# Feed-forward inputs turned and summed in another order, and the opening's Strassen sums taken from turned quarters, in a two-block transformer kernel

## What is computed

```python
def first_block(x, ...):
    h = rms_norm(x, norm_mix); proj = h @ w_in       # 5888 columns: attention, retention, gates
    ...                                              # windowed attention and chunked retention
    x = x + merged @ w_out
    h = rms_norm(x, norm_ffn)
    x = x + (silu(h @ w_gate) * (h @ w_up)) @ w_down # 2816 wide
    return rms_norm(x, final_norm)

def hybrid_layer(x, ...):
    ...                                              # dilated attention and spatial gating
    x = x + rms_norm_2(mix, g_post_mix)
    h = rms_norm_2(x, g_pre_ffn)
    f = jnp.square(jax.nn.relu(h @ w_ff1)) @ w_ff2   # 4096 wide
    return x + rms_norm_2(f, g_post_ffn)
```

## Time and profile before

| | us |
|---|---|
| median of 3 runs | 2594.77 |
| lowest and highest | 2594.12 and 2595.74 |
| the profiled execution | 2595.17 |
| its span in the trace | 2593.3 |
| PE busy | 2550.8 |
| DVE, POOL, ACT busy | 1585.5, 1246.0, 1052.7 |

### The profile page before, as it was taken

How to read it: one execution, slowest core, us unless ns; L and a number is a source line. 1 busy time by engine, 2 the same in 40 slices (tenths; PEclk the granted TensorE clock), 3 DMA queues, 4 the chain that set the end, 5 groups by cost and what they waited for, 6 DMA issues and landing times. The chain is left out here.

```text
span 2593.3 us, 35295 instructions
## 1 busy us (share of the span) xinstructions
PE 2550.8 (98%) x13038; PEld 2127.8 (82%) x13038; DVE 1585.5 (61%) x2592; ACT 1052.7 (41%) x2081; POOL 1246.0 (48%) x994
## 2 busy tenths in 40 slices
PE   8999999999999999999999999999998999999998
PEld 6888888677888888888888878998888888888886
DVE  7355554685536554454698761168658666587787
ACT  4332343584224332232444551169744322254443
POOL 2479784354525665555221774548545544200204
PEclk9999999999999999999999999999999999999999
DMA  5557674705551222222752344323143333364534
GB/s 216 193 185 284 223 263 155 276 18 190 187 184 66 74 89 90 79 77 72 284 191 94 110 151 180 89 65 86 51 132 106 114 106 112 118 250 134 184 102 166
DMA packets 162710, 372.40 MB, mean 144 GB/s; under 512 B 21538, under 2 KB 42658, under 8 KB 158882
## 3 DMA queue, kind: packets, MB, share of 16 engines
q1 hardware_dynamic: 162540, 370.15, 41.5%
HBM read 268.01 MB, written 101.83 MB: 143 GB/s over the span
## 5 line engine op out<-in xcount | busy, mean ns | idle before, releaser
L2353 POOL TENSOR_TENSOR WL<-WRAW,WH 128x512 fp32r<-128x512 f32 (+1 forms) x149 | 247.7, 1664 | 277.2 <-ACT WH L1098 277.1
L852 PE MATMUL PS<-HH,WL 128*128 128x512 f32 (+1 forms) x976 | 368.5, 378 | 2.6 <-DVE HL L1881 0.9
L854 PE MATMUL PS<-HL,WH 128*128 128x512 f32 (+1 forms) x976 | 366.7, 376 | 0.0
L855 PE MATMUL PS<-HH,WH 128*128 128x512 f32 (+1 forms) x976 | 366.6, 376 | 0.0
L1619 DVE TENSOR_TENSOR WL<-TS,WH 128x512 fp32r<-128x512 f32 x228 | 245.6, 1086 | 193.1 <-ACT WH L1098 193.0
L917 PE MATMUL PS<-WH,DAL 128*128 128x512 f32 x756 | 294.7, 390 | 0.0
L919 PE MATMUL PS<-WH,DAH 128*128 128x512 f32 x756 | 294.5, 390 | 0.0
L918 PE MATMUL PS<-WL,DAH 128*128 128x512 f32 x756 | 294.5, 390 | 0.0
L2532 POOL TENSOR_TENSOR X<-X,DV 128x512 f32<-128x512 f32 x56 | 90.1, 1633 | 354.4 <-DVE DV L2024 270.3
L1098 ACT ACTIVATE WH<-TS 128x512 fp32r<-128x512 f32 x228 | 138.3, 621 | 213.9 <-POOL TS L2369 213.8
L2369 POOL TENSOR_TENSOR TS<-WRAW 128x512 f32<-128x512 f32 x114 | 153.2, 1344 | 129.8 <-issue 122.6
(11 more groups left out here) (418 smaller groups left out, 6070.0 us busy)
## 6 DMA issues: line engine op xcount, KB each, us to landing
WRAW<-in_u_f SPq DMA_DIRECT2D x56, 512.0 KB, 3.9
WRAW<-in_u_in SPq DMA_DIRECT2D x54, 512.0 KB, 4.4
WRAW<-scr_t SPq DMA_DIRECT2D x52, 512.0 KB, 3.7
scr_h<-HS SPq DMA_DIRECT2D x96, 256.0 KB, 2.2
WRAW<-in_u_gu SPq DMA_DIRECT2D x44, 512.0 KB, 3.4
scr_t<-TTa SPq DMA_DIRECT2D x18, 1024.0 KB, 4.1
WRAW<-in_u_out SPq DMA_DIRECT2D x24, 512.0 KB, 3.5
scr_x<-X SPq DMA_DIRECT2D x24, 512.0 KB, 4.9
```

What stands on the lines that cost most here:

```text
L852: e.matmul(PS[:, b, 0:wd], wl[:, blk(kk)], op_moving(q, kk, c0, wd, 0), start=(kk == 0), stop=False)
L854: e.matmul(PS[:, b, 0:wd], wh[:, blk(kk)], op_moving(q, kk, c0, wd, 1), start=False, stop=False)
L855: mm = e.matmul(PS[:, b, 0:wd], wh[:, blk(kk)], op_moving(q, kk, c0, wd, 0), start=False, stop=(kk == 3))
L2353: e.tensor_tensor(lo, raw, hi.bitcast(F32), ALU.subtract).then_inc(*c.inc("w_lo_p", i))
```

## The change

In the opening the sixteen transposed sum tiles and turn0 go. POOL writes the whole (high plus low) of the turned quarters of rows 0 to 3 back over X (whole_rows, at i = 0 and 1, behind the low part of weight unit 6); DVE's sums0 forms S3 and S2 from them and from the PSUM banks of the turned rows 4 to 7, which it now frees (before, the split of the row did); POOL forms S4 and S1 at i = 6 to 9; ACT and DVE split the four sums from X, in SBUF, at i = 4 to 15.

In both feed-forward openings four groups (j = 2) move ahead of the first product and the other four (j = 3) to P2 (two), P4 and P3 of block (0, 0). ACT's high parts of the sums are taken out of turn and put in a list of their own, HIGH_TERMS. DVE runs two of the four early groups before the norm of the first block's last row and two after P1, ahead of the low part of the seventh weight operand. POOL's low parts move a little earlier. In the second opening ACT, in place of DVE, squares the quarters of pairs 0 and 1.

```diff
+    HIGH_AT = {4: [("S3", 0), ("S2", 0)], 5: [("S3", 1), ("S2", 1)], 6: [("S3", 2), ("S2", 2)], 7: [("S3", 3), ("S2", 3)],
+               9: [("S4", 0)], 10: [("S4", 1)], 11: [("S4", 2)], 12: [("S4", 3)],
+               13: [("S1", 0)], 14: [("S1", 1)], 15: [("S1", 2), ("S1", 3)]}
+    LOW_AT = HIGH_AT
...
-    AFTER_OUT = {7: 2, 8: 2, 9: 2, 10: 2}
-    AFTER_PROD = {0: [0, 1, 1, 1, 1, 0, 1], 1: [1, 1, 1, 0, 0, 0, 0]}
+    AFTER_OUT = {7: 2, 8: 2, 9: 2, 10: 2, 15: 4}
+    AFTER_PROD = {0: [0, 0, 0, 0, 2, 1, 1], 1: [0] * 7}
...
-    LOW_PROD = {0: [0, 0, 0, 1, 1, 1, 1], 1: [0, 1, 1, 1, 1, 0, 0]}
+    LOW_PROD = {0: [0, 0, 1, 1, 2, 0, 0], 1: [2, 2, 0, 0, 0, 0, 0]}
+    HIGH_TERMS = [(q, j) for j in range(4) for q in ("S1", "S3", "S2", "S4")]
+    HIGH_OUT = {8: 4, 10: 4}
+    HIGH_PROD = {0: [4, 0, 0, 0, 0, 1, 3], 1: [0] * 7}
+    SUMS_OUT = {**AFTER_OUT, 15: 2}
+    SUMS_PROD = {0: [2, 0, 0, 0, 2, 1, 1], 1: [0] * 7}
...
 PE, opening:
-        def turn0(q, j):
-            b = open_bank(("nb", 1, q, j))
-            w.wait_ge(*c.at("s_ov", (1, j, "S4")))
-            for i in range(4):
-                mm = e.transpose(PS[:, b, blk(i)], by_tile(rows0(q, j))[:, i, :], ID[:, :])
-            mm.then_inc(*bk.fill(("nb", 1, q, j)))
...
 ACT, opening:
+        def high_term(q, j):
+            if q == "S4":
+                w.wait_ge(*c.at("s_op", (1, j, "S1")))
+            if q == "S1":
+                w.wait_ge(*bk.full(("rv", 1, j + 4)))
+            w.wait_ge(*sum0_done(q, j))
+            e.activation(op_cols(q, j, 0), whole0(q, j), ACT.Copy).then_inc(*c.inc("h_hi", (1, q, j)))
...
 ACT, second feed-forward:
+        def squared(m, c0, wd, p):
+            t = quarter(2, m, DONE[p])[:, c0:c0 + wd]
+            w.wait_ge(*bk.out((p, 2, m, c0)))
+            e.activation(t, t, ACT.Relu).then_inc(*c.inc("f_r", (m, c0, p)))
+            w.wait_ge(*c.at("f_r", (m, c0, p)))
+            e.activation(t, t, ACT.Square).then_inc(*c.inc("f_s", (m, c0, p)))
...
                     if c0 == 0 and m in AFTER_PROD:
                         turns(k, backs, AFTER_PROD[m][x])
+                        high_terms(k, highs, HIGH_PROD[m][x])
                         if m == 0:
                             split()
+                    if lay == 2 and m < 2 and p in ("P4", "P3"):
+                        squared(m, c0, wd, "P5" if p == "P4" else "P4")
+                        if p == "P3":
+                            squared(m, c0, wd, "P3")
...
 DVE, opening:
+            key = "nb", 1, j + 4, 0
+            for q, b2, left, right in (("S3", 0, whole0("A11", j), None), ("S2", 1, None, whole0("S3", j))):
+                key = "nb", 1, j + 4, b2
+                ps = by_tile(PS[:, bk.at(key), :])
+                e.tensor_tensor(whole0(q, j), ps if left is None else left, ps if right is None else right,
+                                ALU.subtract).then_inc(*bk.free(key))
...
 DVE, first feed-forward:
+            if i == 15:
+                turns(2, backs, SUMS_OUT[i])
             if i in COMPLETE:
                 w.wait_ge(*c.at("gb0", 2))
                 norm(2, tt, GF[:, :])
-            turns(2, backs, AFTER_OUT.get(i, 0))
+            if i < 15:
+                turns(2, backs, SUMS_OUT.get(i, 0))
...
 DVE, second feed-forward:
-                    if lay == 2 and p in ("P5", "P4", "P3"):
+                    if lay == 2 and m >= 2 and p in ("P5", "P4", "P3"):
...
                     if c0 == 0 and m in AFTER_PROD:
-                        turns(k, backs, AFTER_PROD[m][x])
                         if also and m == 0:
                             also(x)
+                        turns(k, backs, SUMS_PROD[m][x])
...
 POOL, opening:
+        def whole_rows(tt):
+            for half in range(2):
+                hh, hl = [t[:, 4 * half:4 * half + 4, blk(tt)].bitcast(F32) for t in (HH, HL)]
+                w.wait_ge(*bk.out(("nb", 1, tt, half)))
+                w.wait_ge(*bk.full(("nb", 1, tt, 1)))
+                e.tensor_tensor(whole0(("A11", "A12")[half], tt), hh, hl, ALU.add).then_inc(*c.inc("s_op", (tt, half)))
...
+            if i < 2:
+                whole_rows(2 * i)
+                whole_rows(2 * i + 1)
+            if 6 <= i < 10:
+                sums0(i - 6)
```

More of the change, by code:

```diff
@@ L611, in op_done @@
     def op_done(k, q, j):
-        return c.at("s_op", (k, q, j)) if k > 1 and q[0] == "S" else bk.out(("nb", k, q, j))
+        if q[0] == "A":
+            return bk.out(("nb", k, q, j))
+        return c.at("s_ov", ("lo", q, j)) if k == 1 else c.at("s_op", (k, q, j))
     def op_cols(q, j, lo):
@@ L703, in normed @@
                 for b2 in range(2):
-                    w.wait_ge(*bk.out(("nb", k, tt, b2)))
+                    w.wait_ge(*(c.at("s_ov", (tt, b2)) if k == 1 and tt > 3 else bk.out(("nb", k, tt, b2))))
         back(1, 0)
@@ L1239, in act_program @@
                         w.wait_ge(*c.at(f"h11_{par(m)}", (0, m - 2)))
+                    else:
+                        for j in range(4):
+                            w.wait_ge(*c.at("s_ov", ("lo", "S1", j)))
                     w.wait_ge(*bk.full(key))
@@ L1281, in turn, with high_terms @@
             e.activation(op_cols(q, j, 0), ps, ACT.Copy).then_inc(*c.inc("h_hi", key))
-            for sq in {"A22": (), "A11": ("S1",), "A12": ("S3", "S2", "S4")}[q]:
-                w.wait_ge(*c.at("s_ov", (k, j, sq)))
-                e.activation(op_cols(sq, j, 0), op_whole(sq, j), ACT.Copy).then_inc(*c.inc("h_hi", (k, sq, j)))
+        def high_terms(k, highs, n):
+            for _ in range(n):
+                q, j = highs.pop(0)
+                w.wait_ge(*c.at("s_ov", (k, j, q)))
+                e.activation(op_cols(q, j, 0), op_whole(q, j), ACT.Copy).then_inc(*c.inc("h_hi", (k, q, j)))
         def turns(k, backs, n):
@@ L1409, in fin1 @@
                 square_g(tt - 1)
-        strassen(1, 2, ACT.Silu, backs)
+        strassen(1, 2, ACT.Silu, backs, highs)
         ffn_down(1, fin1)
@@ L1601, in fin2 @@
             square(6, tt, SS[1][:, tt:tt + 1], SQ[:, :])
-        strassen(2, 4, ACT.Relu, backs, lambda: front3(PO[7]))
+        strassen(2, 4, ACT.Relu, backs, highs, lambda: front3(PO[7]))
         ffn_down(2, fin2)
@@ L1685, in dve_program, with low_term @@
+        def low_term(q, j):
+            w.wait_ge(*c.at("h_hi", (1, q, j)))
+            e.tensor_tensor(op_cols(q, j, 1), whole0(q, j), op_cols(q, j, 0).bitcast(F32),
+                            ALU.subtract).then_inc(*c.inc("s_ov", ("lo", q, j)))
         for i, key in enumerate(RVG):
+            if 3 <= i < 7:
+                sums0(i - 3)
             if 2 <= i < 5:
                 back(1, 3 + i)
-            if 3 <= i < 7:
-                sums0(i - 3)
-            for _ in range(TURN_AT.get(i, 0)):
-                turn0(*turned0.pop(0))
@@ L1692, in dve_program @@
             if i < 15:
                 feed(key)
-        for j in range(4):
-            turn0("S1", j)
+            for q in LOW_AT.get(i, ()):
+                low_term(*q)
         nr, n1 = len(R1), len(A1)
@@ L2288, in dve_program @@
                 variance(4, tt, SS[0], VV[0])
-            turns(4, backs, AFTER_OUT.get(i, 0))
+            turns(4, backs, SUMS_OUT.get(i, 0))
             if i < 15:
@@ L2402, in pool_program, with sums0 @@
         n_split[0] = 6
+        def whole_rows(tt):
+            for half in range(2):
+                hh, hl = [t[:, 4 * half:4 * half + 4, blk(tt)].bitcast(F32) for t in (HH, HL)]
+                w.wait_ge(*bk.out(("nb", 1, tt, half)))
+                w.wait_ge(*bk.full(("nb", 1, tt, 1)))
+                e.tensor_tensor(whole0(("A11", "A12")[half], tt), hh, hl, ALU.add).then_inc(*c.inc("s_op", (tt, half)))
+        def sums0(j):
+            w.wait_ge(*sum0_done("S2", j))
+            e.tensor_tensor(whole0("S4", j), whole0("A12", j), whole0("S2", j), ALU.subtract).then_inc(
+                *c.inc("s_op", (1, j, "S4")))
+            w.wait_ge(*c.at("s_op", (1, j, "S4")))
+            w.wait_ge(*c.at("s_ov", ("lo", "S2", j)))
+            e.tensor_tensor(whole0("S1", j), whole0("S2", j), whole0("A11", j), ALU.add).then_inc(
+                *c.inc("s_op", (1, j, "S1")))
         for i, key in enumerate(RVG):
```

69 lines of the change are left out of this document (23 added, 46 removed).

## The result

The changed kernel took 2599.85 us (median of 14 runs, 2597.02 to 2602.81), the kernel before 2594.48 us beside it (14 runs, 2593.28 to 2595.88): a ratio of 1.0020, with a 95% interval from 1.0012 to 1.0028. It is slower by 5.4 us, inside the predicted range, 3.5 us over the predicted time. The profiled execution took 2598.65 us, 3.5 more than that of before.

What follows compares the result with a forecast made beforehand. PE, busy 2550.8 of 2593.3 us, was taken as the bound. Opening -7.3, first feed-forward opening +3.2 and second +5.6 sum to +1.5 us on the median of 2594.77: 2596.3 us, range 2586.5 to 2601.

Runs made afterwards that it cites:

- ffn_entry: Feed-forward part of the change alone, behind the old opening, with the second layer's j = 2 groups moved behind P6 and P7; 2597.99 us, ratio 1.0012.
- ffn_spread: ffn_entry with the first layer's groups, sums, high and low parts of j = 3 where the kernel before has them; 2593.57 us.
- ffn_alone: Feed-forward part of the change alone, behind the opening of the kernel before; 2602.15 us, ratio 1.0026 to the kernel before.
- after_late: The changed kernel with the eight value transposes one product later, nothing else; 2598.39 us, ratio 1.0014 to the kernel before.
- combined_c: ffn_spread plus j = 3 late in the second layer, and the change's opening with S4, S1 on DVE and value transposes one product later; 2586.27 us.

## What to carry to other kernels

Work taken off the engine that bounds shortens a stage only as far as every loop of the other engines comes forward with it. Look for the consumer with the least slack, and count among the consumers what stands in the same queue behind the late operation, whatever it is for. Price a new wait of PE of some 2 us and more at its own length plus half of several microseconds at 1.2 GHz, and expect that part to differ between executions. A transpose that waits ahead of a product holds the product too: put it behind the products that can already run (5.0 us in ffn_entry, 2.2 of them waits and 3.2 clock), and keep operations that nobody needs yet behind the one that is next to be read (2.7 us in ffn_spread where neither side has half clock, 4.15 against ffn_entry).

## What the runs showed of the hardware

The stretches at half clock were about 3.4, 6.8 and 10.2 us long, behind waits of PE of 2.0 to 4.4 us. The same wait had different stretches in different kernels: 3.0 us for row 6's norm was followed by none in the changed kernel and by 3.4 us in ffn_alone; the 2.0 us at P2' and 1.9 to 2.8 us at P4' by none in the changed kernel, 6.8 us in ffn_entry and 10.2 us in after_late. A stretch that falls beside a wait, as part of the one at 182 us does, costs less than half its length. combined_c is the one of the fourteen traces without a stretch at half clock in either opening: its longest wait in the second is 1.7 us, where every other kernel has one of 2.0 us or more.

A subtraction of DVE over 128x512 with both operands in SBUF took 0.68 us beside an idle POOL. Begun while a POOL operation ran, it mostly ended about 0.55 us after that operation (185 of 208 in the changed kernel), so it took up to 1.8 us in the rows above, and the POOL operation behind it rose from 1.29 to about 1.74 us.
